# 32 bytes between fours of FFN operand tiles, 64 bytes between the slots of the low weight halves

## What is computed

```python
def _conv_ffn(h, w_in, conv_w, conv_b, w_out):
    t = h.shape[1]
    u = h @ w_in                                   # 2048 -> 2 * 5632
    up = jnp.pad(u, ((0, 0), (CONV_WIDTH - 1, 0), (0, 0)))
    c = conv_b + up[:, 0:t] * conv_w[0]
    for j in range(1, CONV_WIDTH):
        c = c + up[:, j:j + t] * conv_w[j]
    gate, val = jnp.split(c, 2, axis=-1)
    return (jax.nn.silu(gate) * val) @ w_out       # 5632 -> 2048
```

## Time and profile before

| | |
|---|---|
| median of 2 runs | 1993.99 us (1993.92 to 1994.06) |
| span of the profiled execution | 1992.6 us |
| PE busy | 1979.7 us, 99% |
| DVE busy | 1418.9 us, 71% |
| ACT busy | 992.0 us, 50% |
| POOL busy | 143.9 us, 7% |

### The profile page before, as it was taken

How to read it: one execution, slowest core, us unless ns; L and a number is a source line. 1 busy time by engine, 2 the same in 40 slices (tenths; PEclk the granted TensorE clock), 3 DMA queues, 4 the chain that set the end, 5 groups by cost and what they waited for, 6 DMA issues and landing times.

```text
span 1992.6 us, 33224 instructions
## 1 busy us (share of the span) xinstructions
PE 1979.7 (99%) x11726; PEld 1746.3 (88%) x11726; DVE 1418.9 (71%) x1969; ACT 992.0 (50%) x1180; POOL 143.9 (7%) x157
## 2 busy tenths in 40 slices
PE   9999999999999999999999999999999999999998
PEld 8998888888888888888899899888888888888886
DVE  6856788877887786554567668788778877865444
ACT  6556445555545554343455654554555555534433
POOL 1112220000000000110120004100000000011000
PEclk9999999999999999999999999999999999999999
DMA  8566655555555555556575445655555556676654
GB/s 299 177 196 161 196 188 189 177 200 191 189 175 193 193 194 192 190 176 205 191 237 179 132 136 179 197 184 178 190 193 195 189 183 196 207 235 213 200 188 137
DMA packets 106870, 379.67 MB, mean 191 GB/s; under 512 B 12107, under 2 KB 12684, under 8 KB 106668
## 3 DMA queue, kind: packets, MB, share of 16 engines
q1 hardware_dynamic: 102332, 362.22, 54.7%
q0 software_dynamic: 4176, 16.07, 3.2%
q10 hardware_dynamic: 288, 0.33, 0.1%
HBM read 368.09 MB, written 10.49 MB: 190 GB/s over the span
## 4 chain that ended last, share of the span: by engine, by line
PE 96%; DVE 2%; DMA 1%; SPq 0%; ACT 0%; issue 0%; ACTq 0%
PE ps L429 46%; PE ps L432 24%; PE ps L823 4%; PE ps L822 4%; PE ps L821 4%; PE ps L723 2%; PE ps L725 2%; PE ps L724 2%; DMA raw<-weights 1%; DVE w_lo L1172 1%; PE ps L761 1%; PE ps L784 1%; PE ps L459 1%; PE ps L460 1%; PE ps L458 1%; PE ps L772 1%
## 5 line engine op out<-in xcount | busy, mean ns | idle before, releaser
L1172 DVE TENSOR_TENSOR w_lo<-raw,w_hi 128x1024 fp32r<-128x1024 f32 (+1 forms) x678 | 824.9, 1230 | 498.5 <-ACT w_hi L861 477.2
L861 ACT ACTIVATE w_hi<-raw 128x1024 fp32r<-128x1024 f32 (+1 forms) x678 | 710.4, 1054 | 778.4 <-PE ps L432 454.9
L429 PE MATMUL ps<-op_in,w_hi 128*128 128x512 f32 x2992 | 1026.4, 391 | 1.7 <-DVE w_lo L1205 0.9
L432 PE MATMUL ps<-op_in,w_lo 128*128 128x256 f32 x2992 | 812.3, 282 | 0.0
L429 PEld LDWEIGHTS ps<-op_in,w_hi 128*128 128x128 f32 x2992 | 548.9, 188 | 106.1 <-issue 1.3
L432 PEld LDWEIGHTS ps<-op_in,w_lo 128*128 128x128 f32 x2992 | 564.8, 189 | 15.7
L429 PE MATMUL ps<-op_ffn,w_hi 128*128 128x512 f32 x704 | 243.1, 390 | 0.0
L432 PE MATMUL ps<-op_ffn,w_lo 128*128 128x256 f32 x704 | 195.8, 282 | 0.0
L429 PEld LDWEIGHTS ps<-op_ffn,w_hi 128*128 128x128 f32 x704 | 131.1, 188 | 26.5
L821 PE MATMUL ps<-w_hi,op_ffn 128*128 128x512 f32 x352 | 139.5, 396 | 0.0
L822 PE MATMUL ps<-w_lo,op_ffn 128*128 128x512 f32 x352 | 139.5, 396 | 0.0
(11 more groups left out here) (218 smaller groups left out, 2052.4 us busy)
## 6 DMA issues: line engine op xcount, KB each, us to landing
raw<-weights SPq DMA_DIRECT2D x662, 512.0 KB, 4.1
raw<-weights SPq DMA_DIRECT2D x16, 384.0 KB, 3.1
bias_rows<-brow POOLq DMA_DIRECT2D x1, 6144.0 KB, 36.1
win_bias<-bias_rows POOLq DMA_DIRECT2D x4, 1024.0 KB, 8.4
h<-xt SPq DMA_DIRECT2D x8, 256.0 KB, 7.2
raw<-weights SPq DMA_DIRECT2D x8, 256.0 KB, 6.2
x_tok<-x_rows SPq DMA_DIRECT2D x4, 512.0 KB, 8.7
h_rows<-h_blocks POOLq DMA_DIRECT2D x16, 128.0 KB, 5.5
```

The source lines that it names most:

```text
L429: return mm(ps[:, bank, 0:2 * T], whi, op, start=start, stop=stop)
L432: return mm(ps[:, bank, 0:T], wlo, op[:, 0, :], start=False, stop=False)
L861: f(w_hi[s][:, 0:cols], raw[s][:, 0:cols], ACT.Copy).then_inc(hi_ready, 1)
L1172: v.tensor_tensor(w_lo[s][:, 0:cols], raw[s][:, 0:cols], w_hi[s][:, 0:cols].bitcast(F32), ALU.subtract).then_inc(lo_ready, 1)
```

## The change

The low halves of the ring become one tensor, in which the slots are 1040 elements apart where they were 1024, so that slot s begins 64 s bytes further on: remainders 0, 64, 0, 64. The operand of each FFN becomes 11 quads of four tiles, and each quad is followed by 8 unused elements (32 bytes): the remainder of quad q is 32 + 32 q in layer 0 and 96 + 32 q in layer 1, taken modulo 128. `par` loses 64 elements that nothing used, which makes up for the ring's 256 bytes: `ident` and everything behind it up to `op_ffn` stay where they were, and `h`, `half_b`, `cg`, `cv`, `up` and `par` move by 256 bytes. The rest is the indexing that goes with it.

```diff
+QUAD = 8 * T + 8
...
-    w_lo = [new(f"w_lo{s}", [P, CH], F32R) for s in range(SLOTS)]
+    ring_lo = new("w_lo", [P, SLOTS, CH + 16], F32R)
+    w_lo = [ring_lo[:, s, 0:CH] for s in range(SLOTS)]
...
-    par = new("par", [P, 7 * P])
+    par = new("par", [P, PC_END])
...
-    rg = region(FT * 2 * T * 4 + 64)
+    rg = region(FT // 4 * QUAD * 4 + 64)
     r_o = rg + 57344
-    op_ffn = [place("op_ffn0", [P, FT, 2, T], F32R, rg), place("op_ffn1", [P, FT, 2, T], F32R, rg + 64)]
+    op_ffn = [place(f"op_ffn{k}", [P, FT // 4, QUAD], F32R, rg + 64 * k)[:, :, 0:8 * T].rearrange(
+        "p q (k s t) -> p q k s t", k=4, s=2) for k in range(2)]
+
+    def four(op, tile0, half):
+
+        if len(op.shape) == 4:
+            return op[:, sl(tile0, 4), half, :]
+        return op[:, sl(tile0.over(4), 1), :, half, :][:, 0, :, :]
+
+    def one(op, kt):
+
+        return op[:, kt, :, :] if len(op.shape) == 4 else op[:, kt // 4, kt % 4, :, :]
...
-                                         op[:, kt0 + k, :, :], first and k == 0, last and k == 1)
+                                         one(op, kt0 + k), first and k == 0, last and k == 1)
...
-                    hi, lo = op_ffn[1][:, kt0 + k, 0, t], op_ffn[1][:, kt0 + k, 1, t]
+                    hi, lo = one(op_ffn[1], kt0 + k)[:, 0, t], one(op_ffn[1], kt0 + k)[:, 1, t]
...
-                            op_high(Lin(k0, 1, i), op_ffn[layer][:, sl(Lin(0, 4, i), 4), 0, :])
+                            op_high(Lin(k0, 1, i), four(op_ffn[layer], Lin(0, 4, i), 0))
...
-                op_low(k, op[:, sl(tile0, 4), 1, :], op[:, sl(tile0, 4), 0, :])
+                op_low(k, four(op, tile0, 1), four(op, tile0, 0))
```

## The result

The changed kernel takes 2004.45 us (median of 2 runs, 2003.64 to 2005.27) against 1993.99: 0.5% slower, ratio 1.0051 with a 95% interval of 1.0034 to 1.0069. The time lies inside the range of the prediction, but its likeliest case, no effect at all, is not what happened. The profiled executions differ by 9.1 us in their spans, 2001.7 against 1992.6.

The account below looks back on a forecast made before the run. The prediction took PE's matmul count times the distance between starts as the bound. All terms were taken as 0, so the span of 1992.6 us plus 1.4 us to the median gave 1994.0 us; range 1983 to 2009.

Parts of the forecast that it names:

- likeliest case: Whole kernel: addresses don't matter to PE, time stays within 3 us of 1994; chance 0.52.
- What bounds the kernel: Whole kernel: number of matmuls times the distance between their starts, plus some 13 us at the two ends.
- chance of 2% either way: Whole kernel: faster by over 2% had chance 0.03, slower by over 2% 0.03, within 2% 0.94.
- Low halves: Ring slots 64 bytes apart, in pairs, triples and row matmuls: taken as 0, bound 14.1 us together, either way.
- sign of being wrong: Feature pairs in odd slots: distance moving by more than a nanosecond would show that addresses count for PE.
- The slower rival: Feature pairs with low halves at 64 run at the token tiles' pace: 14.3 us more, 2008; chance 0.17.
- yardstick of 1.7%: Matmuls of 256 and 512 columns: 1.7% more where weights move than where they are stationary; 5.9 ns a pair.
- Layer 0's quads: Layer 0's FFN operand, read by 704 pairs: taken as 0, bounds +1.9 us and -3.0 us.
- Layer 1's quads: Layer 1's FFN operand, stationary in 1056 matmuls: taken as 0, gain of 1.9 us, at most 4.2 us.
- An unseen remainder that is better: Feature pairs and f1_out: a remainder not in the trace is faster, 22.5 us, 1971, more likely 1983; chance 0.15.
- mirrored yardstick: Feature pairs win 5.9 ns each and f1_out's 1056 matmuls come to 226.3 ns, 8.0 less.
- Splits and the rest: DVE and ACT splits, operand writers, and the moved `h`, `cg`, `cv`, `up` and `par`: costed at 0.

Follow-up runs that it names:

- a3: Against the changed kernel: old ring of low halves, and only layer 1's FFN operand in quads; 1992.3 us, ratio 0.9990 to before.
- b2: Against the kernel with the spaced ring alone: low halves of all slots 64 bytes on, instead of 0, 64, 128, 192; 2013.9 us, ratio 1.0097 to before.
- a4: Against the kernel with the spaced ring alone: low halves at 0, 128, 128 and 256 bytes instead of 0, 64, 128, 192; 1996.7 us, ratio 1.0012 to before.

## Why the prediction was right in its range and wrong in its case

- **What bounds the kernel** held: the time is the number of matmuls times the time between two starts, and only the latter moved. No wait and no other engine took part. That the chance of 2% either way was small held too, in both directions: the slowest kernel here is 1.0% slower, the fastest 0.4% faster.
- **Low halves, taken as 0.** This is the step that failed. I took 0 because f0_in and f0_out had the same pace though they read from different tensors. But both tensors lie at the same distance from the weights, 32, so the two rows were one measurement, not two. In its place the runs show that a low half 192 bytes on costs a pair 6.6 ns and one 64 bytes on 2.6 ns, and that the kernel with the ring alone takes 2004.2 us against 1994.4. The prediction's own sign of being wrong, more than a nanosecond a pair in an odd slot, came true. The other reason, that 32 and 96 had the same 1.7%, was an accident: f1_out has 233.3 ns at 32, 234.3 at 96 and 226.7 at 0, and the token tiles at 32 are another kind of matmul.
- **The slower rival** had the mechanism, that low halves in odd slots slow the feature pairs, and 14.3 us. Measured were 10.5 in all. Per pair it had 5.9 ns in both odd slots; measured were 6.6 in slot 3, 2.6 in slot 1 and 1.5 in slot 0, which the rival left out. It also left out the 2.1 us that f1_out gives back. Its yardstick of 1.7% came from comparing matmuls whose weights move with matmuls whose weights stand. That is not what makes f1_out slow, since the same matmuls take 226.7 ns at distance 0. That the yardstick has the size of the real effect, slow patterns 1 to 2% above the fast one, is luck. So is it that the range, which reaches to 2009 for this rival with its chance of 0.17, takes in 2004.45.
- **Layer 0's quads, taken as 0 within -3.0 and +1.9.** Alone they cost 2.5 us, beyond the upper bound: 5 quads of 11 were counted as exposed, and all 8 that left remainder 32 were.
- **Layer 1's quads, taken as 0 within -4.2 and 0.** They save 2.1 us, inside these bounds. More than half of it comes from quads 3 and 5: in `a3` their 96 matmuls each take 5.0 and 7.2 ns less than before, 1.2 us in the two.
- **An unseen remainder that is better** was there, with the size of my mirrored yardstick: 226.7 ns against the 226.3 that I had worked out for f1_out, and 340.0 ns for a feature pair against 346.6 - 5.9 = 340.7. The change put the operand there only in quad 5 of f1_out and in two chunks of f0_out. The nearness of the sizes is luck here too.
- **Splits and the rest at 0** held: DVE 1419.1 us busy against 1418.9. The 4080 pairs of the prediction leave out 64 that read `op_lat`; half of them at 5.9 ns are 0.2 us.

The section "Who interferes with whom" of "SBUF — State Buffer" in the Trainium skill, by which the sum was 0, agrees with these traces on the other engines (before the change, the chunks between the ends of a group have 173.33 ns a matmul in f0_in and in f0_out, with DVE busy for 16.63 or 8.57 of 20 us). It does not cover what these runs show within PE: moving one of its two operands by 64 bytes, with all else in place, changes its pace by 1.8% (f0_out in `b2`, 248.4 against 243.9 us). As to the cause, a conflict between the reads of the moving operand and of the next weights fits that their distances count, but it is argued and not shown; nothing in the traces shows a single read. Why there are several patterns at one distance, and what picks one, stays open.

## What to carry to other kernels

When a kernel is bound by back-to-back float32 matmuls, the place of the stationary and the moving operand against each other, in steps of 16 to 32 bytes, was worth 1 to 3% of a stage here. Scan it in one run by padding the tiles, read the times between starts and not only the durations, and then give all tiles the best place, instead of spreading them over many. Where two stationary tensors take turns, as the high and low weights do, vary both distances: a scan of one alone missed the fastest combination here. Before two rows are taken as evidence that a property has no effect, look whether the property differs between them. A change that sums to nothing may be two effects; time its parts alone.

## What was not expected of the hardware

- A matmul that moves 512 columns had from 226.7 to 235.5 ns to the next start in the mean of a stage, at one clock and without a wait, by the addresses of its operands. A pair of 512 and 256 columns had 340.0 to 353.4 ns in the mean of at least six.
- The best common distance depends on which operand moves: 0 or 16 bytes in f1_out, where weights move, but 32 or 160 in the feature stages, where 0 costs 176.2 ns a matmul against 173.3. Two chunks at 192 from the high half and 0 from the low one had 170.0.
- After a change of slot in `a4` the old pattern gives way within two to four pairs, and yet two stages of `b2` with the same addresses have 176.4 and 174.5 ns a matmul from their second group to their ends.
